# Mixer B's key and value chunks as one stretch with seven block products for four pairs of row pairs

## The reference

```python
h = rms_norm(x, pre_norm_w[l])
proj = h @ w_in[l]                       # 256 x 4096 by 4096 x C_IN
...
q = rope(q, pos) * (dh ** -0.5)          # mixer B
k = rope(k, pos)
for window, d in DILATIONS:              # (128,1), (512,4), (2048,16)
    num, m, den = band_attention(...)
...                                      # merged by the softmax denominators
```

## Time and profile before

| what | value |
|---|---|
| median of three runs | 1753.71 us |
| the profiled execution | 1754.08 us |
| its span | 1752.3 us |
| TensorE busy | 1744.5 us, 100% |
| VectorE busy | 1253.4 us, 72% |
| ScalarE busy | 922.1 us, 53% |
| GpSimd busy | 597.9 us, 34% |
| TensorE's granted clock | 1.00 in every slice |
| DMA | 344.79 MB, mean 197 GB/s |

### The profile page before, as it was taken

One profiled execution on the slowest core, in us unless ns is written; L12 is line 12 of the kernel. 1 busy time (PEld: TensorE's weight loads), 2 busy tenths in 40 slices (PEclk: granted clock), 3 DMA queues, 4 the chain that ended last, 5 costly groups with the idle time before them and its releaser, 6 DMA issues.

```text
span 1752.3 us, 22441 instructions
## 1 busy us (share of the span) xinstructions
PE 1744.5 (100%) x7839; PEld 1443.8 (82%) x7839; DVE 1253.4 (72%) x1301; ACT 922.1 (53%) x1244; POOL 597.9 (34%) x834
## 2 busy tenths in 40 slices
PE   9999999999999999999999999999999999999998
PEld 7888888888888888888888888888888888888886
DVE  7657656787887878655665567556655786979797
ACT  7544444554554546456445644554455564656564
POOL 2335303367594948730432142324222510000000
PEclk9999999999999999999999999999999999999999
DMA  8876677556565656666666666666666657656575
GB/s 294 244 207 193 193 236 241 170 169 180 156 182 156 180 167 170 184 195 187 178 192 193 192 180 192 192 192 183 185 193 195 177 174 239 205 192 235 179 283 216
DMA packets 181822, 344.79 MB, mean 197 GB/s; under 512 B 14944, under 2 KB 19296, under 8 KB 181216
## 3 DMA queue, kind: packets, MB, share of 16 engines
q1 hardware_dynamic: 181008, 342.58, 65.5%
q10 hardware_dynamic: 720, 0.93, 0.2%
HBM read 339.27 MB, written 4.19 MB: 196 GB/s over the span
## 4 chain that ended last, share of the span: by engine, by line
PE 96%; DVE 2%; ACT 0%; DMA 0%; issue 0%; SPq 0%; ACTq 0%; DVEq 0%
PE acc L728 27%; PE acc L734 26%; PE acc L731 26%; PE acc L987 3%; PE acc L988 3%; PE acc L989 3%; PE acc L906 1%; DVE w_parts L2027 1%; PE heads L987 1%; PE heads L988 1%; PE heads L989 1%; PE scores L895 0%; PE scores L794 0%; DMA raw<-in_w_in 0%; PE scores L827 0%; PE scores L826 0%
## 5 line engine op out<-in xcount | busy, mean ns | idle before, releaser
L1482 DVE TENSOR_TENSOR w_parts<-raw,w_parts 128x1024 fp32r<-128x1024 f32 x526 | 669.1, 1273 | 425.3 <-ACT w_parts L1110 423.8
L1110 ACT ACTIVATE w_parts<-raw 128x1024 fp32r<-128x1024 f32 x526 | 556.5, 1058 | 527.9 <-PE acc L734 514.0
L728 PE MATMUL acc<-w_parts,x_parts 128*128 128x512 f32 x2048 | 800.5, 391 | 0.5 <-DVE w_parts L1482 0.3
L734 PE MATMUL acc<-w_parts,x_parts 128*128 128x512 f32 x2048 | 797.6, 389 | 0.0
L731 PE MATMUL acc<-w_parts,x_parts 128*128 128x512 f32 x2048 | 797.0, 389 | 0.0
L734 PEld LDWEIGHTS acc<-w_parts,x_parts 128*128 128x128 f32 x2048 | 384.4, 188 | 81.1 <-DVE x_parts L1524 0.3
L728 PEld LDWEIGHTS acc<-w_parts,x_parts 128*128 128x128 f32 x2048 | 384.6, 188 | 79.7 <-issue 1.3
L731 PEld LDWEIGHTS acc<-w_parts,x_parts 128*128 128x128 f32 x2048 | 384.6, 188 | 78.5
L604 POOL COPY rot<-tok_b 32x256 f32<-32x256 f32 x120 | 86.9, 724 | 140.6 <-DVE tok_b L1856 135.7
L588 POOL TENSOR_TENSOR rot<-tok_a,trig 128x512 f32<-128x512 f32 x18 | 30.6, 1698 | 260.6 <-ACT tok_a L1116 121.4
L987 PE MATMUL acc<-w_parts,x_parts 128*128 128x512 f32 x229 | 89.1, 389 | 0.0
(11 more groups left out here) (302 smaller groups left out, 1711.5 us busy)
## 6 DMA issues: line engine op xcount, KB each, us to landing
raw<-in_w_in SPq DMA_DIRECT2D x478, 512.0 KB, 3.6
blocks_raw<-in_w_out SPq DMA_DIRECT2D x96, 512.0 KB, 5.0
raw<-in_w_out SPq DMA_DIRECT2D x32, 512.0 KB, 4.1
raw<-in_w SPq DMA_DIRECT2D x16, 512.0 KB, 4.7
x_tok<-in_x SPq DMA_DIRECT2D x4, 1024.0 KB, 8.9
xt_raw<-in_x_t SPq DMA_DIRECT2D x7, 512.0 KB, 6.3
wpost<-in_post_w SPq DMA_DIRECT2D x4, 512.0 KB, 5.6
out<-y SPq DMA_DIRECT2D x4, 512.0 KB, 2.7
```

The source lines that it names most:

```text
L728: nc.tensor.matmul(o, stat_hi, mov_hi, start=(k == 0), stop=False)
L734: last = nc.tensor.matmul(o, stat_lo, mov_hi, start=False, stop=(k == KB - 1))
L1110: nc.scalar.activation(w_hi[:, n % SPLIT_SLOTS, :, 0:width], raw[:, n % RAW_SLOTS, :, 0:width], ACT.Copy).then_inc(hi_ready, 1)
L1482: V.tensor_tensor(w_lo[:, s, :, 0:width], raw[:, n % RAW_SLOTS, :, 0:width], w_hi[:, s, :, 0:width].bitcast(F32), ALU.subtract).then_inc(l ...
```

## The change

The key and value chunks of a group become one stretch of 32 positions, as `joint_place` says. Positions 0 to 3 are the key columns of row pairs 4 to 7. For i from 0 to 3, position 4+4i holds the key columns of row pair i and position 5+4i its value columns; positions 6+4i and 7+4i are the key columns of row pairs 8+2i and 9+2i. Positions 20 to 31 are the value columns of row pairs 4 to 15. So the keys are complete after position 19.

Each pair of positions 4+4i, 5+4i is a unit: its 2x2 blocks are multiplied by seven products in place of eight, three of them straight from the ring, four with sums of weight blocks that VectorE makes ahead of position m and splits behind position m+2; only half of position m+1 is split. Sums of x blocks for all four units (`joint_sums`) are made once, in the query chunk of group 0. Products that belong to several results collect in the free banks (`heads`, `scores`, `trans`) and are added, scaled and combined behind the keys and behind the values.

The rotation, transposition and moves of the keys come later with them; the moves run on into the gate chunk. B's scores, softmax and first probabilities come five positions later, the second probabilities and both value products in the next chunk (ahead of positions 5 and 6). Some tiles are placed anew, and the counts of semaphores that the output projection shares are shifted.

```diff
+N_JOINT = 4
+UNITS_JOINT = GROUPS * N_JOINT
+JOINT_UNITS = {4 + 4 * i: i for i in range(N_JOINT)}
+LATE_SHIFT = 5
+JOINT_STEPS = {8: 0, 13: 1}
+JOINT_HI_STEPS = {10: (0, 1), 15: (2, 3)}
+JOINT_LO_STEPS = {12: (0, 1), 15: (2, 3)}
+KEYS_OUT = LEAD + 1
+def joint_place(m):
+    if m in JOINT_UNITS:
+        return JOINT_UNITS[m], 0
+    if m - 1 in JOINT_UNITS:
+        return JOINT_UNITS[m - 1], 1
+    if m in JOINT_PLAIN:
+        return JOINT_PLAIN[m], 0
+    return m - PAIRS, 1
...
 # sync: weight transfers
-                load_chunk(w_in_v, C_B + 1 + 4 * g, KBC + NC * g)
-                load_chunk(w_in_v, C_B + 2 + 4 * g, VB + NC * g)
+                for m in range(2 * PAIRS):
+                    n, j = joint_place(m)
+                    first = sp.snap((VB if j else KBC) + NC * g)
+                    sp.wait_ge(lo_ready, 16 * (C_B + 1 + 4 * g) + m - RAW_SLOTS + 1)
+                    sp.dma_start(raw[:, m % RAW_SLOTS, :, :], w_in_v[:, 2 * n:2 * n + 2, bass.ds(first, NC)]
+                                 ).then_inc(raw_landed[m % RAW_SLOTS], 16)
...
 # TensorE
+                def unit(m, i):
+                    start, stop = i == 0, i == N_JOINT - 1
+                    unit_no = N_JOINT * g + i
+                    pe.wait_ge(lo_ready, 16 * c + m + 1)
+                    product(acc[:, 1, 0, :], x_block(2 * i + 1, 0), ring(m, 1), False, False)
+                    if start:
+                        pe.wait_ge(heads_taken, TILES * (GROUPS + g))
+                        pe.wait_ge(s_ready, N_JOINT)
+                    product(heads[:, 0, :], x_block(2 * i, 0), ring(m, 0), start, stop).then_inc(weights_used, 1)
+                    pe.wait_ge(lo_ready, 16 * c + m + 2)
+                    if start:
+                        pe.wait_ge(acc0_free, c)
+                    product(acc[:, 0, 0, :], joint_block(i, 3), ring(m + 1, 1), start, False).then_inc(weights_used, 1)
+                    plain_position(m + 2)
+                    pe.wait_ge(sums_13_ready, unit_no + 1)
...
+                    product(trans[:, :], joint_block(i, 2), part_13[1], start, stop)
+                    product(heads[:, 1, :], joint_block(i, 0), part_13[0], start, stop).then_inc(sums_13_used, 1)
+                    pe.wait_ge(sums_24_ready, unit_no + 1)
+                    product(scores[:, :], joint_block(i, 1), part_24[0], start, stop)
+                    product(acc[:, 1, 1, :], x_block(2 * i + 1, 1), part_24[1], False, False).then_inc(sums_24_used, 1)
+                    plain_position(m + 3)
+                for m in range(N_JOINT):
+                    plain_position(m)
+                for m, i in JOINT_UNITS.items():
+                    unit(m, i)
+                for m in range(PAIRS + N_JOINT, 2 * PAIRS):
+                    plain_position(m)
...
-                    if g > 0 and n == 0:
-                        pair_values(1, g - 1)
+                    if g > 0 and n in (LATE_SHIFT, LATE_SHIFT + 1):
+                        pair_values(n - LATE_SHIFT, g - 1)
...
 # ScalarE, attention_b_frames
+                for m in range(LEAD, 2 * PAIRS + LEAD):
+                    at = m - LEAD
+                    if 6 <= at <= 13:
+                        move_turned(at - 6, g, 0)
...
+                    if 27 <= at <= 31:
+                        move_turned(at - 27, g, 1)
+                    if m - 1 in JOINT_UNITS:
+                        split_half(c, m)
+                    else:
+                        split(c, m)
+                    if m - 2 in JOINT_UNITS:
+                        unit_sums(JOINT_UNITS[m - 2], g)
...
 # VectorE
+            def unit_sums(c, m, i, g):
...
+                V.tensor_tensor(sum_13[:, :, :], b12.broadcast_to([P, 2, NC]), b11_b22, ALU.subtract).then_inc(sums_13_made, 1)
+                dve.wait_ge(sums_13_made, unit_no + 1)
...
+                V.tensor_tensor(sum_24[:, 0, :], b22, sum_13[:, 0, :], ALU.subtract).then_inc(sum_2_made, 1)
+                dve.wait_ge(sum_2_made, unit_no + 1)
+                V.tensor_tensor(sum_24[:, 1, :], b21, sum_24[:, 0, :], ALU.subtract).then_inc(sums_24_made, 1)
+            def unit_rests(i, g):
...
+            def extra_results(g):
+                dve.wait_ge(u_moved, g + 1)
+                dve.wait_ge(sums_24_used, N_JOINT * (g + 1))
+                V.tensor_tensor(e_4, scores[:, :], e_1, ALU.add).then_inc(u_step, 1)
...
+            def combine_scaled(dst, parity, extras):
+                for t in range(TILES):
+                    V.scalar_tensor_tensor(dst[t], acc[:, parity, t, :], r[t], extras[t], ALU.mult, ALU.add
+                                           ).then_inc(acc0_free if t == 0 else acc1_free, 1)
...
             def attention_b_frames(g, mixing=()):
+                for m in range(LEAD, 2 * PAIRS + LEAD):
+                    at = m - LEAD
...
+                    if m in JOINT_UNITS:
+                        unit_sums(c, m, JOINT_UNITS[m], g)
+                    if m - 1 in JOINT_UNITS:
+                        split_half(c, m)
+                    else:
+                        split(c, m)
+                    if m - 2 in JOINT_UNITS:
+                        unit_rests(JOINT_UNITS[m - 2], g)
+                    if at == PAIRS + KEYS_OUT - 1:
+                        extra_results(g)
+                    if at in (5, PAIRS + KEYS_OUT + 6):
+                        j = at // PAIRS
+                        dve.wait_ge(rope_done, TILES_ROTATED + 2 + 2 * j + 4 * g)
+                        V.transpose(tok_a[:, :, :], rot[:, :, :]).then_inc(b_turned, 1)
```

More of the change, by code:

```diff
@@ new lines, in product, with x_block, ring @@
+            def product(bank, stat, mov, start, stop):
+                nc.tensor.matmul(bank, stat[0], mov[0], start=start, stop=False)
+                nc.tensor.matmul(bank, stat[0], mov[1], start=False, stop=False)
+                return nc.tensor.matmul(bank, stat[1], mov[0], start=False, stop=stop)
+            def x_block(k, t):
+                return x_hi[:, k, t * P:(t + 1) * P], x_lo[:, k, t * P:(t + 1) * P]
+            def ring(m, kk):
+                return w_hi[:, m % SPLIT_SLOTS, kk, :], w_lo[:, m % SPLIT_SLOTS, kk, :]
@@ L1280, in mixing_frame @@
                     at = n - LEAD
+                    if later is not None and at == LATE_SHIFT - 3:
+                        later_probs(later, 1)
+                    if summed and at in JOINT_HI_STEPS:
+                        for i in JOINT_HI_STEPS[at]:
+                            joint_first(i)
                     if turned is not None and at in LATE_TURN_STEPS:
@@ new lines, in move_turned, with split_half @@
+            def move_turned(step, g, j):
+                rows, half = divmod(step, 2)
+                act.wait_ge(b_turned, 2 * g + j + 1)
+                dst = qrot_t[:, :, :] if j == 0 else k_t[:, 0, :, :]
+                for cols in (2 * half, 2 * half + 1):
+                    last = move_quarters(tok_a, dst, rows, cols)
+                if step == 7:
+                    last.then_inc(b_moved, 1)
+            def split_half(c, n):
+                act.wait_ge(raw_landed[n % RAW_SLOTS], 16 * (PAIRS // RAW_SLOTS * c + n // RAW_SLOTS + 1))
+                act.wait_ge(weights_used, 16 * c + (n - SPLIT_SLOTS + 1))
+                nc.scalar.activation(w_hi[:, n % SPLIT_SLOTS, 1, :], raw[:, n % RAW_SLOTS, 1, :], ACT.Copy
+                                     ).then_inc(hi_ready, 1)
@@ L1395, in sums_first @@
             def sums_first(q, i, slot, made, used, ready):
[L1397 removed]
+                act.wait_ge(made, UNITS_JOINT + seven(q, i) + 1)
                 if i > 0:
[L1399 removed]
+                    act.wait_ge(used, UNITS_JOINT + seven(q, i))
                 elif q > 1:
@@ L1870, in turn_mixed, with sum_x, make_joint @@
                                         ).then_inc(heads_taken, TILES)
-            def mixing_frame(c, group, of_a):
+            def sum_x():
+                V.tensor_tensor(x_sum[:, :, :, :].rearrange("p k t q -> p k (t q)"), x_hi[:, 0:2 * N_JOINT, :].bitcast(F32),
+                                x_lo[:, 0:2 * N_JOINT, :].bitcast(F32), ALU.add).then_inc(x_summed, 1)
+            def make_joint(b):
+                pairs = x_sum[:, 4 * b:4 * b + 4, :, :].rearrange("p (i two) t q -> p i two t q", two=2)
+                a11, a21 = pairs[:, :, 0, 0, :], pairs[:, :, 0, 1, :]
+                a12, a22 = pairs[:, :, 1, 0, :], pairs[:, :, 1, 1, :]
+                out = [joint_sums[:, :, m, :] for m in range(4)]
+                dve.wait_ge(x_summed, 1)
+                if b > 0:
+                    dve.wait_ge(s_ready, 2 * b)
+                V.tensor_tensor(out[0], a21, a22, ALU.add).then_inc(s_step, 1)
+                V.tensor_tensor(out[2], a21, a11, ALU.subtract).then_inc(s_step, 1)
+                dve.wait_ge(s_step, 3 * b + 1)
+                V.tensor_tensor(out[1], out[0], a11, ALU.subtract).then_inc(s_step, 1)
+                dve.wait_ge(s_step, 3 * b + 3)
```

(30 more changed lines are left out.)

289 lines of the change are left out of this document (183 added, 106 removed).

## The result

The changed kernel takes 1769.8 us in the median (1768.1 to 1770.2, four runs) against 1753.7 us: a ratio of 1.009, 95% interval 1.0072 to 1.0107. It is slower, as forecast, but by 16.1 us where the forecast had 9.4, and above the range of 1750 to 1767.

The account below looks back on a forecast made before the run. TensorE, busy 1744.5 of 1752.3 us, was taken as the bound. Fewer matmuls save 10.9 us and waits for the late transposition cost 20.3, so +9.4 on 1753.7 gives 1763.1 us; range 1750 to 1767.

Parts of the forecast that it names:

- The mechanism: Key stretch, units 0 and 1: rotation delays VectorE's transposition, ScalarE stands for it, TensorE loses 5.1 us per group, 20.3 in all.
- S: Start of key position 0 in a group's key stretch; 734.15 in group 0 of the kernel before.
- the delay ends at position 10: Key stretch: TensorE waits in pieces at positions 8, 9 and 10; after that nothing more should be lost.
- X - 17.2: Loss per group in us, zero below that; with 2.72 saved per group, the change pays while X is under S+19.9.
- X: Start of the queries' transposition on VectorE, counted from S: forecast S+22.3, where it was S+16.0 before.
- 12.1: VectorE's own queue from S+3.35 to the transposition: 8 operations of 1024 and 5 of 512, 12.1 us.
- the 6.8: Nine of GpSimd's ten rotation operations fall into VectorE's dense queue and add their full length, 6.8 us.
- its unit of 0.2267 us: Time of one matmul in TensorE's stream, from 12 matmuls per position of 2.72 us in group 0's key and value chunks.
- Costed at nothing: Joint sums of x (bounds 0 and 2 us), combining key results, five-position shift, second move of probabilities, transfers: all taken as 0.
- 10.9 were saved: TensorE: four units in four groups save 48 matmuls of 0.2267 us, 10.9 us.
- The rotation costs no more than now: Rival: rotation costs VectorE's queue 1.8 us, X = S+17.3, loss 0 to 0.4 us a group, 1743 to 1744.5; chance 0.17.
- Half of it is taken beside idle moments: Rival: rotation adds 3.8 to 5.6 us to VectorE's queue, loss 2.0 to 3.8 us a group, 1751 to 1758; chance 0.18.
- The delay doesn't end at position 10: Rival: ScalarE's spare 0.8 us per unit is used up, 0.5 us lost in each of two units, four groups; 1767; chance 0.08.

Follow-up runs that it names:

- the kernel with the rotation cut short: Changed kernel, but GpSimd rotates one of 64 columns of B's queries with the same number of instructions: 1748.3 us, ratio 0.9969.
- the kernel with TensorE kept busy: Changed kernel with 9 and 8 more matmuls in unit 1 of each group where TensorE waits, 68 in all: 1762.2 us, ratio 1.0048.
- weights from x: Later-turned kernel, but the unit products take blocks of x in place of the joint sums, which are still made: 1745.5 us, ratio 0.9952.
- later-turned kernel: Changed kernel with the transposition of the queries at position 7 instead of 5 and ScalarE's moves at 9 to 16 instead of 6 to 13: 1747.0 us.
- the one with ScalarE's order changed: Later-turned kernel, but ScalarE takes the joint sums' first parts behind the probabilities' part and the weight copy in group 0's query chunk: 1748.9 us.

## Why the prediction was off

**The mechanism held, step by step.** VectorE's queue is dense from S+3.4 to the transposition, GpSimd and VectorE take turns (1.76 us for 1.22), ScalarE stands for the transposition with positions 9 and 10 behind it, and the delay ends at position 10: units 2 and 3, the gate chunks and position 20 and after have no wait. By the Trainium skill, "SBUF — State Buffer", "Who interferes with whom", the port pair that VectorE and GpSimd share is an exclusive lock. This trace agrees in the main: the operations beside the rotation start 1.68 us apart, and in the kernel with the rotation cut short 1.15. If each waited out the whole of the other, it would be 1.14 + 0.73 = 1.87.

**The size of the delay.** Forecast: transposition at S+22.3, loss 5.1 us a group. Measured: S+21.2 and 4.0. The formula X - 17.2 gives exactly that for 21.2; X itself was 1.1 too late. The queue took 755.94 - 738.14 = 17.8 us, and 18.9 was forecast (12.1 + 6.8). The term at fault is the 6.8. Nine of the rotation's operations did fall into the queue, as forecast, and nine of VectorE's are stretched, from 738.14 to 750.54. But each turn added less than the 0.70 us that the forecast took (0.73 less 0.03): beside a 256-wide rotation it is 1.68 - 1.14 = 0.54 us, and beside the 512-wide one 1.11 (745.50 - 743.79 for an operation that hands on after 0.60) where 1.26 was taken. The nine added 5.4 us, and 0.2 more went in the sums' waits for each other behind the rotation: 17.8 - 12.1 = 5.7. This error alone would have made the forecast 4.4 us too high; it hid part of what was missing.

**The missing term.** What failed is the step that made a wait cost only its own length. The waits here are followed by matmuls at the lower clock, some 8 us in all (7.6 at the least, by the kernel with TensorE kept busy). The prediction took its unit of 0.2267 us from a kernel in which TensorE never waits, and never asked what a wait does to it. This is what carried the time out of the range: less 8 us, the measured 1769.8 would be 1761.8, near the forecast 1763.1. That nearness is luck in part: the delay was forecast 4.4 us too long, and the joint sums and the pace were left out.

**Costed at nothing.** The joint sums cost 0.9 us in waiting. Their bounds were 0 to 2, so the range had it; the value was wrong because it leaned on the window 865 to 913, a query chunk of a later group, with GpSimd busy 11 of 48 us. The sums are made in group 0's query chunk, where mixer A's last group is still being finished and GpSimd is busy 34 of 44. Wrong stretch, right kind of row. The five positions of shift cost nothing by a run of their own. For the combining, the transfers and the second move of probabilities there is none, but TensorE has no wait where they lie. Not in the prediction at all: the pace of 0.2275 to 0.2325 us, 1.5 us by the comparison of weights from x.

**The balance.** The span grew by 15.6 us and 10.9 were saved, so 26.5 were lost: 4 x 4.0 = 16 in waits, some 8 by the clock, 0.9 at the joint sums, and 1.5 by the pace. These make 26.4, and a few tenths either way are within what such a count can tell. In the later-turned kernel the same terms are 1.4 + 0.9 + 1.5 = 3.8 of its 4.2 us.

**The rivals.** "The rotation costs no more than now" promised 1743 to 1744.5. With hardly any rotation the kernel took 1748.3, so that rival was priced too low too: VectorE would have waited for ScalarE's copies, and joint sums and pace stay. "Half of it is taken beside idle moments" is nearest in the waits (4.0 us against its upper 3.8, 5.7 in the queue against its upper 5.6), but not for its reason: the queue had no idle time, each turn was shorter. "The delay doesn't end at position 10" is nearest in time, 1767, but its mechanism isn't in the trace.

## What to carry over

When a change makes TensorE wait, count the wait and then look at what the clock does behind it: here the clock added half as much again to the waits (8 us to 16), and only in part of the runs when there was one long wait per group. Where a transposition comes late, let nothing that TensorE needs soon stand behind it on another engine: with the moves put off by two or three positions, and in the second case the transposition by two, the same change went from 16 us slower to 4 and to 6.8 us faster. Take the bound for added work from the stretch where it will be done, with the same neighbours on GpSimd, not from one that merely has the same name.

## What the runs showed of the hardware

- Behind a single wait of 1.67 us per group the granted clock fell to its lower level in all four groups of the profiled run (mean granted clock 0.996), while five other runs of the same kernel have 0.999 or 1.000; behind two of 1.74 and 1.50 us, 2.5 us apart, it fell in all four groups of the profiled run. Behind waits of up to 0.7 us in the query and key chunks (718.2 in the changed kernel, 749.3 in the one with ScalarE's order changed) it did not fall in any trace here. The Trainium skill, "TensorE: Matmul & The Clock Gate", Part 1, tells that the throttled state is the default and that activity releases it. The trace agrees with that as far as it goes: 9 and 8 extra matmuls in the waits kept the higher level throughout.
- At granted clock 1.00 matmuls of the same shape, with blocks of x as the units' weights in both cases, followed each other in 0.2315 us with these weights in the joint buffers and in 0.2270 with them in x's own, but only behind a gap in the stream; ahead of it, both keep 0.2267.
- GpSimd's copies, with one input, are held up by VectorE's two-input operations too: sixteen copies 32x128 took 8.65 us or 11.95 by what VectorE did beside them.
